# Two transformer blocks in fp32 from split products: where in SBUF the rows of h, m and the pooled values begin

## The reference

```python
h = rms_norm(x, ffn_pre_g) * (1.0 + sc2) + sh2          # end of block 1
y = (silu(h @ w_gate) * (h @ w_up)) @ w_down            # 2048 -> 5632 -> 2048
...
m = sigmoid(g_attn) * (attn @ w_attn_o) + sigmoid(g_pool) * (pool @ w_pool_o)
mix = m @ w_out                                         # block 2, mixer
...
a = causal_dwconv(h @ w_up, conv_w, conv_b)             # block 2, 2048 -> 11264
gate, val = split(a, 2)
y = (gelu(gate) * val) @ w_down
```

## Time and profile before

| what | before |
|---|---|
| median of the runs | 2712.65 us |
| the profiled execution, its own time | 2716.24 us |
| its span, first to last instruction | 2714.4 us |
| TensorE matmul busy (PE) | 2606.1 us, 96% |
| VectorE busy | 1705.6 us, 63% |
| ScalarE busy | 1220.3 us, 45% |
| mean granted TensorE clock | 0.984 of 2.4 GHz |

### The profile page before, as it was taken

One profiled execution on the slowest core, in us unless ns is written; L12 is line 12 of the kernel. 1 busy time (PEld: TensorE's weight loads), 2 busy tenths in 40 slices (PEclk: granted clock), 3 DMA queues, 4 the chain that ended last, 5 costly groups with the idle time before them and its releaser, 6 DMA issues.

```text
span 2714.4 us, 53794 instructions
## 1 busy us (share of the span) xinstructions
PE 2606.1 (96%) x21278; PEld 2481.6 (91%) x21278; DVE 1705.6 (63%) x2393; ACT 1220.3 (45%) x1649; POOL 49.5 (2%) x98
## 2 busy tenths in 40 slices
PE   5799999899999999999899999999899999999997
PEld 1488888899999999999889899999899999999997
DVE  1388864686666666657755655555676666666667
ACT  1343454544444444445544454444454444444444
POOL 0000000000000000000000000000000000000000
PEclk9799999999999999999999999999999999999999
DMA  9988867476666666565444445555455555555553
GB/s 380 371 320 302 274 217 274 156 269 200 196 199 196 198 196 198 179 186 179 138 149 140 139 146 180 184 181 181 142 179 186 184 186 184 183 185 184 186 178 132
DMA packets 137087, 545.51 MB, mean 201 GB/s; under 512 B 15120, under 2 KB 17424, under 8 KB 124560
## 3 DMA queue, kind: packets, MB, share of 16 engines
q1 hardware_dynamic: 127312, 474.08, 54.0%
q0 software_dynamic: 9216, 67.11, 7.0%
q10 hardware_dynamic: 448, 2.75, 0.3%
HBM read 541.78 MB, written 2.10 MB: 200 GB/s over the span
## 4 chain that ended last, share of the span: by engine, by line
PE 89%; DVE 5%; ACT 3%; DMA 2%; issue 1%; ACTq 0%; DVEq 0%; SPq 0%
PE bank L1612 20%; PE bank L1614 19%; PE bank L1613 19%; PE bank L1749 8%; PE bank L1751 8%; PE bank L1750 8%; PE bank L1648 2%; DMA ada_pre<-in_ada_w 2%; DVE w_lo L1000 2%; ACT w_hi L522 1%; PE bank L1689 1%; DVE y L1065 1%; ACT h_hi L598 1%; DMA bf<-in_f_bias 1%; PE bank L1707 0%
## 5 line engine op out<-in xcount | busy, mean ns | idle before, releaser
L1000 DVE TENSOR_TENSOR w_lo<-raw,w_hi 128x1024 fp32r<-128x1024 f32 x836 | 1012.7, 1224 | 724.5 <-ACT w_hi L522 723.5
L522 ACT ACTIVATE w_hi<-raw 128x1024 fp32r<-128x1024 f32 x836 | 872.6, 1056 | 911.1 <-PE bank L1614 528.5
L1612 PE MATMUL bank<-h_hi,w_hi 128*128 128x258 f32 (+2 forms) x4112 | 1174.8, 286 | 28.9 <-DVE h_lo L1071 20.3
L1613 PE MATMUL bank<-h_lo,w_hi 128*128 128x258 f32 (+2 forms) x4112 | 1169.2, 284 | 0.0
L1614 PE MATMUL bank<-h_hi,w_lo 128*128 128x258 f32 (+2 forms) x4112 | 1169.1, 284 | 0.0
L1612 PEld LDWEIGHTS bank<-h_hi,w_hi 128*128 128x128 f32 x4112 | 785.6, 191 | 46.5 <-DVE h_lo L1071 21.8
L1613 PEld LDWEIGHTS bank<-h_lo,w_hi 128*128 128x128 f32 x4112 | 785.7, 191 | 0.1
L1614 PEld LDWEIGHTS bank<-h_hi,w_lo 128*128 128x128 f32 x4112 | 785.4, 191 | 0.0
L1749 PE MATMUL bank<-hid_hi,w_hi 128*128 128x256 f32 x1280 | 356.0, 278 | 0.0
L1751 PE MATMUL bank<-hid_hi,w_lo 128*128 128x256 f32 x1280 | 355.9, 278 | 0.0
L1750 PE MATMUL bank<-hid_lo,w_hi 128*128 128x256 f32 x1280 | 355.9, 278 | 0.0
(11 more groups left out here) (225 smaller groups left out, 2642.6 us busy)
## 6 DMA issues: line engine op xcount, KB each, us to landing
raw<-in_w_in SPq DMA_DIRECT2D x208, 512.0 KB, 4.2
raw<-in_w_ffn_up SPq DMA_DIRECT2D x176, 512.0 KB, 4.3
ada_raw<-in_ada_w POOLq DMA_DIRECT2D x64, 1024.0 KB, 7.1
raw<-in_w_gate SPq DMA_DIRECT2D x88, 512.0 KB, 4.2
raw<-in_w_up SPq DMA_DIRECT2D x88, 512.0 KB, 4.1
raw<-in_w_down SPq DMA_DIRECT2D x88, 512.0 KB, 4.2
raw<-in_w_ffn_down SPq DMA_DIRECT2D x88, 512.0 KB, 4.3
ada_pre<-in_ada_w SPq DMA_DIRECT2D x32, 1024.0 KB, 8.6
```

The source lines that it names most:

```text
L522: act.activation(w_hi[:, slot], raw[:, slot], ACT.Copy).then_inc(hi_ready, 1)
L1000: dve.tensor_tensor(w_lo[:, slot], raw[:, slot], fp(w_hi[:, slot]), ALU.subtract).then_inc(lo_ready, 1)
L1612: pe.matmul(dst, wh, x_hi(kt), start=first and k == 0, stop=False)
L1613: pe.matmul(dst, wh, x_lo(kt), start=False, stop=False)
```

## The change

Only offsets change; every instruction, its shape and its order stay.

| tile | offset before | first byte read, past a multiple of 256 | offset after | then |
|---|---|---|---|---|
| h 0, `SF` (feed-forward 1) | 128 | 192 | 184 | 248 |
| h 1, `every` (272 columns) | 192 | 192 | 192 | 192 |
| h 1, `ST` (gates) | 192 | 248 | 192 | 248 |
| h 2, `ST` (feed-forward 2) | 136 | 192 | 192 | 248 |
| m | 192 | 192 | 248 | 248 |
| pooled values | 192 | 192 | 248 | 248 |

```diff
-        h_hi = [rows(f"h_hi{n}", "hhi", off, KT) for n, off in enumerate((128, 192, 136))]
-        h_lo = [rows(f"h_lo{n}", "hlo", off, KT) for n, off in enumerate((128, 192, 136))]
+        h_hi = [rows(f"h_hi{n}", "hhi", off, KT) for n, off in enumerate((184, 192, 192))]
+        h_lo = [rows(f"h_lo{n}", "hlo", off, KT) for n, off in enumerate((184, 192, 192))]
...
-        m_hi = rows("m_hi", "r1", 192, KT)[:, :, 0:LIVE]
+        m_hi = rows("m_hi", "r1", 248, KT)[:, :, 0:LIVE]
...
-        m_lo = rows("m_lo", "r2", 2 * AT * ALL * 4 + 192, KT)[:, :, 0:LIVE]
+        m_lo = rows("m_lo", "r2", 2 * AT * ALL * 4 + 248, KT)[:, :, 0:LIVE]
...
-        pl_hi = rows("pl_hi", "r3", 192, AT)[:, :, 0:LIVE]
-        pl_lo = rows("pl_lo", "r3", AT * ROW * 4 + 192, AT)[:, :, 0:LIVE]
+        pl_hi = rows("pl_hi", "r3", 248, AT)[:, :, 0:LIVE]
+        pl_lo = rows("pl_lo", "r3", AT * ROW * 4 + 248, AT)[:, :, 0:LIVE]
```

## The result

The kernel after takes 2698.39 us (median of 6 runs, 2697.01 to 2702.07) against 2711.24 us for the kernel before (6 runs beside it, 2708.89 to 2715.76). The ratio is 0.9947 with a 95% interval of 0.9935 to 0.9959, so 14.4 us less, between 11 and 18. The forecast was 2695.7 us and 17.0 less. A second series of 6 runs, beside 17 of the kernel before (median 2711.34 us), gave 2698.02 us and 0.9946 (0.9932 to 0.9961).

The account below looks back on a forecast made before the run. TensorE's matmul pace was taken to bound the kernel. Moved reads save 17.4 us, less 0.4 for products awaiting h, hid unchanged: 2712.65 - 17.0 = 2695.7 us, range 2688 to 2708.

Parts of the forecast that it names:

- The bound: Whole kernel: TensorE's matmuls, busy for 96% of the span, set the time by the distance between their starts, not by waits.
- The pace of the moved reads: 258-column reads of h, m and pooled values, moved from 192 to 248: 362.5 to 357.1 ns a triple, 17.4 us saved.
- the pool's own halves: Two halves of the pool's own weights read the pooled values' tile: 16 triples, 0.1 us saved.
- The deduction for the heads: First two products of each feed-forward part follow the arrival of h: at most 0.7 us not saved, 0.4 taken off.
- Writes, clock, other engines: Writes at 248 cost the same (at most 1.6 us); clock stays full; VectorE rises to 69%, ScalarE to 47%, nothing late.
- Hid: `down` products, 256 columns at 192, with two pace levels: no change taken; all fast 6.5 us less, all slow 11.4 more.
- a different pace ahead may tip hid: `down` products: a level is something the stream falls into, so a changed pace in preceding products may switch it.
- The gates are quick for something else: Gate products owe their pace to a tile written 272 columns wide and other neighbours, not the byte: no gain, 2712.7; chance 0.06.
- levels at 248 too: Moved matmuls may fall to 369.8 ns a triple: 2708 if part of the stream (chance 0.04), 2731 if most (0.04).
- a plateau at 192 without levels: Part of a rival: 258-column matmuls at 192 sit at 120.8 ns each in both feed-forward parts, which hides the two levels.
- The rule on lines of 16 bytes: SBUF reads cost per 16-byte line; 192 and 248 both touch 65 lines, so the change buys nothing: 2712.65 us.

Follow-up runs that it names:

- Feed-forward 1 put back: The kernel after with h of feed-forward 1 read from 192 again, the rest left at 248; 2704.65 us (12 runs), ratio to the kernel before 0.9976.
- 8 bytes ahead of a multiple of 64: The kernel after with feed-forward 1 read from 56, feed-forward 2 from 120, m from 56, the pooled values from 184; 2704.45 us.
- Odd multiples of 4: The kernel after with feed-forward 1 read from 220, feed-forward 2 from 236, m from 60, the pooled values from 124; 2688.80 us.
- Multiples of 64: The kernel after with feed-forward 1 read from 0 past a multiple of 256, feed-forward 2 from 128, m from 0, the pooled values from 64; 2715.82 us.

## Why the prediction was right

**The bound.** Right. TensorE was and stays without a gap in both loops, and every time above follows from paces.

**The pace of the moved reads.** Right to the nanosecond in the long runs: 362.5 became 357.1 in four places. The sum of 17.4 us was 0.4 too large, because it took 362.5 for every triple from 192, and 168 of them stood at 360.0 in the same trace. The 0.1 us for the pool's own halves is too small to be seen. The forecast rested on gates that already read from 248 in the trace before, and setting them beside the others at the same clock, in the same loop, was enough. The undone part (feed-forward 1 alone back at 362.5, the rest at 357.1) shows that the offset is the cause.

**The deduction for the heads.** Right in kind, but too small. The whole head of a part, 192 triples, didn't shorten by its 1.0 us: the two profiles of the kernel after have 81.1 and 82.6 us for 81.3 in feed-forward 1, and 80.1 and 78.5 for 78.8 in feed-forward 2. So some 2 us of the 17.4 didn't arrive, where 0.4 had been taken off. With a spread of 1.5 us between two executions the term can't be sized better.

**Writes, clock, other engines.** Right: for 258 columns, which is feed-forward 2, line 598 stands at 499 ns and line 1071 at 485, as in the earlier trace rows; feed-forward 1 writes rows of 256 columns, in 498 and 485 ns after 498 and 482. The other engines kept up, and the loops' granted clock is 1.00 in the rows below, which answer to the earlier trace rows.

```profile
core 0: us, PE busy (x) PEld busy (x) DVE busy (x) ACT busy (x) POOL busy (x), PEclk, DMA share, GB/s
...
600.00:1080.00 480.00, 480.00 (x4101) 480.00 (x4101) 305.44 (x350) 201.44 (x228) 3.70 (x7) 1.00 0.65 203
...
2000.00:2600.00 600.00, 600.00 (x5125) 600.00 (x5125) 416.21 (x572) 282.67 (x355) 0.00 (x0) 1.00 0.59 187
```

VectorE is busy for 416.2 of 600 us, 69% as forecast.

**Hid.** "No change" was a choice between two ends (6.5 us less, 11.4 more) and not a mechanism; the ends would have been 6.8 and 11.9 with the levels' exact distance of 13.3 ns. In the first profile of the kernel after hid gained 3.4 us against the one execution before. That the time came within 3 us of the forecast is in this term luck. The remark that a different pace ahead may tip hid was not borne out by the part put back.

**The missing 2.6 us.** The ratio says 14.4 us (the medians 12.9), less than 17.0. Two terms can account for it, and the runs don't separate them. The heads and the 168 triples leave 15.0 of the 17.4. And hid may cost more than before: both profiles of the kernel after have the last two `down` products of each part at the upper level, 256 triples x 13.3 = 3.4 us. For the kernel before there is one profile, and its execution (2716.24 us) was 5 us above the median of the runs (2711.24), which fits its 8 products at the upper level being the exception. That is inferred: no profile of an ordinary execution before was taken.

**The rivals.** "The gates are quick for something else" is refuted by all four moved places. Of "levels at 248 too" the premise was right and the price wrong. In three experiments with the weights in their old place 24 gate triples from 248 ran at 360.1, while the gates of the loop stood at 357.1. But all runs of 64 triples and more from 248 stood at 357.1, and the slow pace lies 3.0 ns above the other, not the 12.7 that were carried over from hid. Nor was there a plateau at 192 without levels: it shows 360.0 beside 362.5. Moving the weights gave a third pace at 248, 363.3.

**The rule on lines of 16 bytes.** What the runs show is that the quickest start, 252, isn't the one with the fewest lines: 252 to 1284 touches 66, 192 and 248 touch 65. The Trainium skill, "SBUF — State Buffer", section Specifications (TRN2), says that each crossing into a new line costs. By that rule, as an estimate, 252 would have been slower than both. It runs at 346.7 ns against 362.5 and 357.1, so the measurement decides against the rule for this stream. Nor is it the larger count that makes 252 quick: reads from 60 touch 66 lines too and run at 360.0.

## What to carry to other kernels

Where TensorE streams without a gap, read its pace from the starts and compare equal shapes at different addresses; a difference inside one trace is worth more than a rule. The start of the streamed tile is then a parameter to sweep in steps of 4 bytes, a different one for each number of columns: here 252 was best of 17 for 258 columns, 192 the best of five tried for 256, and 192 the better of two for 272. Several starts can be tried in one run, one for each tile. Look at every stretch of a stage, since one start can show two paces. The weights' place is a parameter as well, and the best start has to be found again when it changes.

## What the runs showed of the hardware

The pace for 258 columns of float32, ns for three matmuls with their weight loads, by the byte past a multiple of 256 at which the read begins, weights at 0. Bytes are counted from the start of the arena, and the code rounds that start up to a multiple of 32 only; whether it lies at a multiple of 256 in SBUF itself isn't known.

| byte | pace | byte | pace | byte | pace |
|---|---|---|---|---|---|
| 0 | 360.0; 362.5 | 128 | 366.7; 360.0 | 236 | 360.0 |
| 56 | 357.8; 360.0 | 184 | 359.8 | 240 | 357.1 |
| 60 | 360.0 | 188 | 350.0; 350.7 | 244 | 360.0 |
| 64 | 356.0 | 192 | 362.5; 360.0 | 248 | 357.1; 360.1 |
| 120 | 360.0; 353.4 | 220 | 350.0; 360.1 | 252 | 346.7 |
| 124 | 365.8 | 232 | 354.2 | | |

(64, 124, 184 and 232 come from runs of 16 triples between other products. Of two values the first is that of most triples of a feed-forward part or the gates; the second of 56 is that of m, and for 188 the two are m and the pooled values.)

So 258 columns have more than one pace from the same byte too, in the same stage, with the same instructions. The lines show it for 192 in feed-forward 1 and 2 (kernel before), 248 in the gates ("Feed-forward 1 put back"), 120 in feed-forward 2 ("8 bytes ahead of a multiple of 64"), 220 in feed-forward 1 ("Odd multiples of 4"), and for 0 in feed-forward 1 and 128 in feed-forward 2 ("Multiples of 64"):

```profile
L1614 PE MATMUL bank<-h_hi,w_lo x64: 283/283/283, 1126.2 to 1148.9; 128*128 128x258 f32 x64
...
L1614 PE MATMUL bank<-h_hi,w_lo x104: 278/283/283, 1978.7 to 2015.8; 128*128 128x258 f32 x104
...
L1614 PE MATMUL bank<-h_hi,w_lo x24: 278/282/284, 1532.3 to 1540.5; 128*128 128x258 f32 x24
...
L1614 PE MATMUL bank<-h_hi,w_lo x104: 279/279/285, 1969.7 to 2006.1; 128*128 128x258 f32 x104
...
L1614 PE MATMUL bank<-h_hi,w_lo x64: 281/282/284, 1104.5 to 1127.2; 128*128 128x258 f32 x64
...
L1614 PE MATMUL bank<-h_hi,w_lo x192: 277/283/288, 1166.6 to 1235.8; 128*128 128x258 f32 x192
...
L1614 PE MATMUL bank<-h_hi,w_lo x104: 282/284/284, 1972.4 to 2009.5; 128*128 128x258 f32 x104
```

By the exact starts these are 360.0 and 360.0 (192), 360.1 (248), 353.4 (120), 360.1 (220), 362.5 (0) and 360.0 (128) ns for three, all without a gap and at a granted clock of 1.00. Within each of these stretches the pace stays the same. Reads from 252 ran at 346.6 to 347.0 in every gap-free run of 64 triples or more, in five profiles and in three stages.

For 256 columns: 192 at 340.0 or 353.3, 64 at 353.3, 252 at 352.5, 0 at 359.8, 248 at 360.1. For 272: 192 at 370.0, 196 at 380.1. No rule found fits these. The Trainium skill, "TensorE: Matmul & The Clock Gate", section Back-to-back issue gap, gives N/2.4 + 2.5 ns for the isolated gap of one matmul, a function of the columns alone: as an estimate 110.0 for 258, and so 330 for three. It says too that in a stream with weight loads both operations set the spacing. The runs have 346.7 to 366.7 with the weights in one place. They differ by 5.8% at one N, so the columns alone don't give the pace.

What the stream and the weight loads do to each other stays open. In one run the weights' own offset acted (363.3 for 357.1, hid at 355.0) while 252 kept its pace; why, and why one byte has two paces, wasn't shown. It was also not tried whether the paces of 258 columns hold at other row distances than 1280 bytes.
